# Who writes the low parts of the weight units during the two attentions

## The chip, the cores and the metric

One core of a Trainium2 chip runs the whole program. The time is device microseconds of one execution, from launch to end on that core.

## The reference

Two transformer blocks in a row, batch 1, 512 tokens, width 1024, all in float32. What matters here is the start of each block.

- Block 1: `h = rmsnorm(x)`, `proj = h @ w_in`. The first part of `proj` feeds a dilated window attention (12 heads in 3 groups), the second, after a shift by one token (`f + (f_prev - f) * mu`), an RWKV-7 scan, the third the gates. Then `merged @ w_out`, norm, and a feed-forward of 4096.
- Block 2: `proj = rms_norm(h) @ w_in`. It feeds a multiscale pooling, a banded attention with 8 query heads and a sink logit, and the gates. Then `merged @ w_out` and a gated feed-forward of 2816.

```python
logits = einsum(q, k) * scale + bias
p = exp(logits - lse); o = einsum(p, v)                    # block 1
p = exp(scores - m); denom = sum(p) + exp(sink - m)        # block 2
proj = h @ w_in                                            # both: float32 products
```

## The kernel before

**Weights.** All weights come as 126 units of 128 x 2048 float32 (1 MB), in a ring of three slots. A float32 product is made from three products of reduced precision: each unit is split into a high part and a low part, `w = hi + lo`, and so are the activations; line 524 multiplies high by high, 525 high by the activations' low part, 526 low by high. ScalarE writes the high part (`hi`, line 1092), GpSimd the low part, `raw - hi`, in place of the raw unit (line 515, all units in order but for ten). TensorE waits for it with `pe.wait_ge(*low_part(n))`. Ten units (20 to 29) in the RWKV stage have their low part from VectorE (`weights_low`, line 1738). Two semaphores count the low parts, `lo_ready` for GpSimd's and `lo_dve` for VectorE's.

**Order.** The order of each engine's work is written out by hand and each engine runs its own instructions strictly in that order; semaphores join them.

**The attentions.** Both run over items, one head and 128 queries each: 16 in the first attention (4 query tiles x 4 heads of the three groups, 384, 768, 1024, 1280 logits in turn), 32 in the second (256 or 384 logits). Per item:
- TensorE: the logits of item i+1, a fill of side work, *wait for the normalised logits of item i* (`prob_ready`), their transposes (line 601), a second fill, and the product with the values (line 609). The fills are pieces of weight products: 4 + 4 per item of the side columns (RWKV and gates) in the first attention, 2 + 2 per item of the gate columns in the second. A unit lasts two items in the first and four in the second.
- VectorE: scale and bias of the logits (1661, 1658), maximum (1665), for the second attention the sink (1667), the negated maximum (1668); then the hook `beside(i)`; then it waits for the exponential, adds the sink term (1672, second attention), takes the reciprocal (1673) and scales (1674), which releases the transposes. In the first attention the hook is `shift_item` (the token shift of a finished half, lines 1695 and 1696, at items 1 to 9 but for item 6); in the second it runs one step of the pooling.
- ScalarE: copies the transposes (1156), exponentials of item i+1 (1146, with a table load where the function before was another), a hook for the side work (1215, 1222, 1231 and 1528), the item's output (1162), and last the hook `after(i)`. In `after(i)` it writes the high part of a unit: at odd i of the first attention the unit `UNIT0["lora"] + i // 2 + 2` (so 11 after item 1, ..., 18 after item 15), at i = 3, 7, ..., 31 of the second the unit `UNIT0["gatep"] + i // 4 + 2` (78 after item 3, ..., 85 after item 31).

Of the kernel before, what the change touches and what calls it, by code (L numbers as in the profile page):

```python
# [12 lines left out]
ALU = mybir.AluOpType  # L13
# [30 lines left out]
RING = 3  # L44
# [12 lines left out]
UNIT0, USE0, UNITS, USES = {}, {}, {}, {}  # L57
# [108 lines left out]
def build(nc, x, wpack, lora_wa, lora_g, params, rel_bias, post_gains, sink, ctab, btab, icount, out):  # L166
# [7 lines left out]
    with ExitStack() as ctx:  # L174
        top = [nc.sbuf_base + (-nc.sbuf_base) % 64]

        def place(name, shape, dt=F32, at=None):
            size = 4 * int(np.prod(shape[1:]))
            if at is None:
                at = top[0]  # L180
                top[0] += size + (-size) % 64
            return nc.alloc_sbuf_tensor_at(name, shape, dt, offset=at), at + size + (-size) % 64

        def fixed(name, shape, dt=F32):
            return place(name, shape, dt)[0]
# [12 lines left out]
        def sem(name):  # L198
            return ctx.enter_context(nc.semaphore(name))
# [10 lines left out]
        raw = fixed("w_raw", [P, RING, UNIT])  # L210
        Wl = place("w_lo", [P, RING, UNIT], F32R, at=top[0] - 4 * RING * UNIT)[0]
        Wh = fixed("w_hi", [P, RING, UNIT], F32R)
# [106 lines left out]
        hi_ready, lo_ready, lo_dve = sem("hi_ready"), sem("lo_ready"), sem("lo_dve")  # L319
# [57 lines left out]
        source = packed_order()  # L377


        DVE_LO0, DVE_LO1 = UNIT0["rwkv"] + 2, UNIT0["rwkv"] + UNITS["rwkv"]  # L380

        def low_part(n):

            if n < DVE_LO0:
                return lo_ready, n + 1
            if n < DVE_LO1:
                return lo_dve, n - DVE_LO0 + 1
            return lo_ready, n + 1 - (DVE_LO1 - DVE_LO0)


        def half(pair, part):
# [30 lines left out]
        def f32(ap):  # L422
            return ap.bitcast(F32)

        def bank(b, n=512):
            return ps[:, b, 0:n]
# [27 lines left out]
        for h in range(Q_HEADS2):  # L454
            for qt in range(NT):
# [4 lines left out]
                n = (hi - lo) * P  # L460
# [7 lines left out]
        att = [dict(items=items1, LG=LG1, PT=PT1, first=0, banks=(7, 3), out_bank=2, outs=1),  # L468
               dict(items=items2, LG=LG2, PT=PT2, first=len(items1), banks=(6,), out_bank=7, outs=4)]
# [15 lines left out]
        @block.sync  # L485
        def _(sp):
            def load(n):
                if n >= RING:
                    sp.wait_ge(*freed[n - RING])
                sp.dma_start(raw[:, n % RING, :], wpack[source[n]]).then_inc(unit_in[n % RING], 16)  # L490

            xt = x.rearrange("(t p) d -> t p d", p=P)
            sp.dma_start(Xr[:, 0, :], xt[0]).then_inc(x_in[0], 16)
            sp.dma_start(C[:, 0:EARLY], ctab[:, 0:EARLY]).then_inc(ident_in, 16)
            for t in range(1, NT):
                sp.dma_start(Xr[:, t, :], xt[t]).then_inc(x_in[t], 16)
            sp.dma_start(PR[:], params).then_inc(params_in, 16)
            load(0)
            sp.dma_start(RB[0:N_BUCKETS, :], rel_bias).then_inc(rel_in, 16)
            sp.dma_start(BT[:], btab).then_inc(bucket_in, 16)  # L500
            load(1)
            sp.dma_start(C[:, EARLY:], ctab[:, EARLY:N_EARLY_CCOLS]).then_inc(consts_in, 16)
            for n in range(2, N_UNITS):
                load(n)

        @block.gpsimd
        def _(pool):


            for n in range(N_UNITS):  # L510
                if DVE_LO0 <= n < DVE_LO1:
                    continue
                slot = n % RING
                pool.wait_ge(hi_ready, n + 1)
                nc.gpsimd.tensor_tensor(Wl[:, slot, :], raw[:, slot, :], f32(Wh[:, slot, :]),  # L515
                                        ALU.subtract).then_inc(lo_ready, 1)
# [1066 lines left out]
        def _(dve):  # L1583
            order = Order(dve, dve_order)
            v = nc.vector
# [60 lines left out]
            def attention(a, beside):  # L1646

                items, first, LG = a["items"], a["first"], a["LG"]
                for i, it in enumerate(items):
                    st = 16 + 8 * (i % 2)  # L1650
                    mx, nmx, total, es, rec = (stat[:, st + c:st + c + 1] for c in range(5))
                    dve.wait_ge(lg_full, first + i + 1)
                    if i >= 2:
                        dve.wait_ge(pt_full, items[i - 2]["chunk1"])
                    for s in it["segs"]:
                        dst = LG[:, i % 2, s["off"]:s["off"] + s["n"]]
                        if "slope" in s:
                            ins = v.scalar_tensor_tensor(dst, s["bias"], s["slope"], bank(s["bank"], s["n"]),
                                                         ALU.mult, ALU.add)
                        else:  # L1660
                            ins = v.scalar_tensor_tensor(dst, bank(s["bank"], s["n"]), HD ** -0.5, s["bias"],
                                                         ALU.mult, ALU.add)
                    ins.then_inc(lg_read, 1)
                    dve.wait_ge(lg_read, first + i + 1)
                    order(v.reduce_max(mx, LG[:, i % 2, 0:it["n"]], AX.X))
                    if "sink" in it:
                        order(v.tensor_tensor(mx, mx, SNK[:, it["sink"]:it["sink"] + 1], ALU.max))
                    v.tensor_scalar(nmx, mx, -1.0, None, ALU.mult).then_inc(nmx_ready, 1)
                    beside(i)
                    dve.wait_ge(exp_ready, first + i + 1)  # L1670
                    if "sink" in it:
                        order(v.tensor_tensor(total, total, es, ALU.add))
                    order(v.reciprocal(rec, total))
                    v.tensor_scalar(LG[:, i % 2, 0:it["n"]], LG[:, i % 2, 0:it["n"]], rec, None,
                                    ALU.mult).then_inc(prob_ready, 1)
# [16 lines left out]
            def shift(n, dst, b, buf, mu):  # L1692

                dve.wait_ge(staged, n)
                v.scalar_tensor_tensor(dst[:, 1:T], ps[:, b, 1:T], OM[:, mu:mu + 1], buf[:, 0:T - 1], ALU.mult, ALU.add)
                v.tensor_scalar(dst[:, 0:1], ps[:, b, 0:1], OM[:, mu:mu + 1], None, ALU.mult).then_inc(shifted, 1)  # L1696
                dve.wait_ge(shifted, n)

            def shift_item(i):

                n = i - 1
                if n in (0, 1):
                    shift(n + 1, LTMP[:, n, :], n, G0[:, n, :], 24 + n)
                elif 2 <= n < GATE0 and n % 4 != 1:
                    pair, part = (n - 2) // 4, (n - 2) % 4
                    shift(2 + 3 * pair + part + 1, RKV[:, pair, part, :], n % 2, G0[:, n % 2, :], 8 * part + pair)
# [23 lines left out]

            def inc(ins, name):
                ins.then_inc(rs[name], 1)

            def weights_low(n):
                if DVE_LO0 <= n < DVE_LO1:
                    slot = n % RING
                    dve.wait_ge(hi_ready, n + 1)
                    v.tensor_tensor(Wl[:, slot, :], raw[:, slot, :], f32(Wh[:, slot, :]), ALU.subtract).then_inc(lo_dve, 1)

            def parts(c):  # L1740
                return (RKV[:, c % 2, j, :] for j in range(3))
# [300 lines left out]
            def pooling():  # L2042

                for g in range(4):
                    cur = Zp[:, g, :]
                    for lvl in range(g + 1):
                        left, right = (1, 0) if lvl == 0 else (2 ** (lvl - 1), 2 ** (lvl - 1))
                        dst = PW[:, lvl % 2, :]
                        order(v.tensor_tensor(dst[:, a0:b0], cur[:, a0 - left:b0 - left], cur[:, a0 + right:b0 + right],
                                              ALU.add))  # L2050
                        yield
                        cur = dst
                    mean = PW[:, (g + 1) % 2, 16:16 + T]
                    order(v.tensor_tensor(mean, cur[:, 16:16 + T], IC[:, g, :], ALU.mult))
                    yield
                    order(v.tensor_tensor(mean, mean, Zp[:, g, 16:16 + T], ALU.subtract))
                    yield
                    order(v.tensor_copy(PDh[:, g, :], mean))
                    yield
                    v.tensor_tensor(PDl[:, g, :], mean, f32(PDh[:, g, :]), ALU.subtract).then_inc(pd_ready, 1)  # L2060
                    dve.wait_ge(pd_ready, g + 1)
                    yield
# [1 line left out]
            dve.wait_ge(sink_in, 16)  # L2064
            dve.wait_ge(dist_in, 16)
            pool_work = pooling()
            attention(att[1], lambda i: next(pool_work, None))
            assert next(pool_work, None) is None
            for u in range(2):
                d = USE0["group"] + u  # L2070
# [106 lines left out]
```

## Time and profile before

| | us |
|---|---|
| median of three runs | 2262.39 (2260.95 to 2273.01) |
| profiled execution | 2259.61 |
| its span | 2257.8 |
| TensorE busy | 2058.6 (91%) |
| weight loads of TensorE busy | 1662.7 (74%) |
| VectorE busy | 856.9 (38%) |
| ScalarE busy | 791.4 (35%) |
| GpSimd busy | 533.4 (24%) |

PE is TensorE's matmuls, PEld its weight loads, DVE VectorE, ACT ScalarE, POOL GpSimd. A transpose is a matmul too, and the start of its weight load is when it could begin. The span is from the first to the last instruction; the execution's own time is 1.8 us longer. A row of a timeline gives the start and how long it took; what stands in brackets is the idle time before it and what ended it.

### The profile page before, as it was taken

How to read it: one execution, taken by the hardware profiler on the slowest of the kernel's cores; microseconds unless marked ns; L12 is line 12 of the kernel's file. 1: busy time of each engine (PE TensorE's matmuls, PEld its weight loads, DVE VectorE, ACT ScalarE, POOL GpSimd, SP SyncE). 2: the span in 40 equal slices, each digit the busy share in tenths (PEclk: the TensorE clock that was granted, in tenths of full speed). 3: DMA queues.
4: the chain of work that ended last, by engine and by line, in shares of the span. 5: the costliest groups of instructions: out<-in, count | busy, mean ns of one | idle time of the engine just before them, and what ended most of it. 6: DMA issues, size and time to landing. Idle time of an engine off the chain costs nothing.

```text
span 2257.8 us, 24099 instructions
## 1 busy us (share of the span) xinstructions
PE 2058.6 (91%) x10212; PEld 1662.7 (74%) x10212; DVE 856.9 (38%) x1437; ACT 791.4 (35%) x1140; POOL 533.4 (24%) x120
## 2 busy tenths in 40 slices
PE   6999969999999988998799989989988889999897
PEld 5877747778777877876688778767666677888786
DVE  2023335666666656522411144341553322111243
ACT  4235634435434423312422222242555223222222
POOL 2422210000000000013244434423122423444342
PEclk9999976989999886679799999989999998999999
DMA  4611210101001002013122222222111222322231
GB/s 150 221 56 61 80 63 1 45 21 43 27 22 45 24 20 98 1 47 112 65 93 94 98 89 94 94 79 80 40 55 59 91 69 74 108 95 93 75 97 71
DMA packets 31279, 160.77 MB, mean 71 GB/s; under 512 B 3103, under 2 KB 5535, under 8 KB 14916
## 3 DMA queue, kind: packets, MB, share of 16 engines
q1 hardware_dynamic: 19244, 135.40, 17.7%
q10 hardware_dynamic: 11928, 23.83, 3.1%
q8 instruction: 81, 1.33, 0.2%
q14 instruction: 26, 0.21, 0.0%
HBM read 152.63 MB, written 10.25 MB: 72 GB/s over the span
## 4 chain that ended last, share of the span: by engine, by line
PE 81%; DVE 9%; ACT 6%; issue 2%; POOL 1%; DMA 0%; POOLq 0%; ACTq 0%; DVEq 0%
PE ps L524 21%; PE ps L525 20%; PE ps L526 20%; PE ps L838 2%; PE ps L840 2%; PE ps L830 2%; PE ps L609 2%; PE ps L587 2%; ACT w_hi L1092 2%; POOL w_lo L515 1%; DVE level L1811 1%; PE ps L880 1%; PE ps L601 1%; DVE ht_lo L1602 1%; PE ps L870 1%
## 5 line engine op out<-in xcount | busy, mean ns | idle before, releaser
L515 POOL TENSOR_TENSOR w_lo<-w_raw,w_hi 128x2048 fp32r<-128x2048 f32 x116 | 533.2, 4597 | 1693.9 <-ACT w_hi L1092 1693.9
L524 PE MATMUL ps<-ht_hi,w_hi 128*128 128x512 f32 x1240 | 520.9, 420 | 36.7 <-DVE rkv L1696 22.3
L525 PE MATMUL ps<-ht_lo,w_hi 128*128 128x512 f32 x1240 | 496.9, 401 | 0.0
L526 PE MATMUL ps<-ht_hi,w_lo 128*128 128x512 f32 x1240 | 496.7, 401 | 0.0
L1092 ACT ACTIVATE w_hi<-w_raw 128x2048 fp32r<-128x2048 f32 x126 | 241.3, 1915 | 547.0 <-PE ps L526 532.3
L524 PEld LDWEIGHTS ps<-ht_hi,w_hi 128*128 128x128 f32 x1240 | 240.0, 194 | 119.3 <-issue 44.0
L526 PEld LDWEIGHTS ps<-ht_hi,w_lo 128*128 128x128 f32 x1240 | 240.5, 194 | 53.2
L525 PEld LDWEIGHTS ps<-ht_lo,w_hi 128*128 128x128 f32 x1240 | 241.2, 195 | 43.7 <-issue 1.4
L524 PE MATMUL ps<-w_hi,hid_hi 128*128 128x512 f32 x432 | 171.7, 397 | 24.2 <-DVE hid_lo L2026 16.4
L525 PE MATMUL ps<-w_lo,hid_hi 128*128 128x512 f32 x432 | 170.7, 395 | 0.0
L526 PE MATMUL ps<-w_hi,hid_lo 128*128 128x512 f32 x432 | 170.5, 395 | 0.0
L2026 DVE TENSOR_TENSOR hid_lo<-hidden,hid_hi 128x1024 fp32r<-128x1024 f32 x27 | 114.4, 4249 | 146.7 <-ACT hid_hi L1450 146.7
L524 PEld LDWEIGHTS ps<-w_hi,hid_hi 128*128 128x128 f32 x432 | 82.9, 192 | 43.3 <-issue 17.2
L524 PE MATMUL ps<-w_hi,ht_hi 128*128 128x512 f32 (+2 forms) x256 | 89.9, 351 | 25.4 <-DVE ht_lo L1991 17.6
L1314 ACT ACTIVATE tinv_t<-ps 128x512 fp32r<-128x512 f32 x96 | 57.7, 601 | 116.4 <-PE ps L840 116.4
L526 PEld LDWEIGHTS ps<-w_hi,hid_lo 128*128 128x128 f32 x432 | 82.7, 191 | 17.6
L525 PEld LDWEIGHTS ps<-w_lo,hid_hi 128*128 128x128 f32 x432 | 82.9, 192 | 17.2
L525 PE MATMUL ps<-w_lo,ht_hi 128*128 128x512 f32 (+2 forms) x256 | 89.3, 349 | 0.0
L526 PE MATMUL ps<-w_hi,ht_lo 128*128 128x512 f32 (+2 forms) x256 | 89.1, 348 | 0.0
L1811 DVE TENSOR_TENSOR level<-gram_inv,consts 128x512 fp32r<-128x512 f32 x112 | 80.4, 759 | 0.6
L2021 DVE TENSOR_TENSOR hidden<-ps,gate_act 128x1024 f32<-128x1024 f32 x16 | 19.6, 1224 | 159.9 <-ACT gate_act L1492 159.9
L1833 DVE TENSOR_TENSOR xinv<-ps,consts 128x512 fp32r<-128x512 f32 x96 | 62.4, 683 | 44.9 <-PE ps L830 44.4
(253 smaller groups left out, 2814.0 us busy)
## 6 DMA issues: line engine op xcount, KB each, us to landing
w_raw<-in_wpack SPq DMA_DIRECT2D x126, 1024.0 KB, 4.9
bias_skewed_dram<-bias_rows_dram ACTq DMA_DIRECT2D x1, 3840.0 KB, 22.9
toe<-bias_skewed_dram ACTq DMA_DIRECT2D x1, 3072.0 KB, 14.5
gate_dram<-gate_tile ACTq DMA_DIRECT2D x10, 256.0 KB, 4.8
x_res<-in_x SPq DMA_DIRECT2D x4, 512.0 KB, 6.7
merged<-gate_dram ACTq DMA_DIRECT2D x1, 2048.0 KB, 9.1
gate<-gate_dram ACTq DMA_DIRECT2D x1, 2048.0 KB, 14.1
x_res<-in_x ACTq DMA_DIRECT2D x1, 2048.0 KB, 9.9
```

The costliest lines, as they stand in the source:

```text
L515: nc.gpsimd.tensor_tensor(Wl[:, slot, :], raw[:, slot, :], f32(Wh[:, slot, :]), ALU.subtract).then_inc(lo_ready, 1)
L524: mm(dst, wh, ah, start=first, stop=False)
L525: mm(dst, wh, al, start=False, stop=False)
L526: return mm(dst, wl, ah, start=False, stop=last)
L587: last = mm(bank(s["bank"], s["n"]), s["q"], s["k"], start=True, stop=True)
L609: last = mm(out_slot(a, i), v, PT[:, j, :], start=j == 0, stop=j == len(it["vals"]) - 1)
L830: last = mm(ps[:, 4 + h, tok(t)], Mb[h][:, t, :], Tb[h][:, t, :] if lv else identR[:], start=True, stop=True)
L1092: actf(Wh[:, n % RING, :], raw[:, n % RING, :], ACT.Copy).then_inc(hi_ready, 1)
L1314: actf(TT[h][:].rearrange("p a b -> p (a b)"), bank(6 + h), ACT.Copy)
L1811: inc(v.tensor_tensor(Mb[h][:], GA[h][:], lmask(lv), ALU.mult), "m_ready")
L1833: inc(v.tensor_tensor(Xb[h][:], b3(4 + h), cast4(ident), ALU.add), "x1_ready")
L2026: v.tensor_tensor(HIl[:, 2 * g:2 * g + 2, :], HID[:, 2 * g:2 * g + 2, :], f32(HIh[:, g % RING, :, :]), ALU.subtract).then_inc(hid_lo, 1)
```

## The change

The units whose low part VectorE writes are now a list: units 11 to 17 in the first attention, 20 to 29 as before, 78 to 84 in the second. GpSimd skips them. In the first attention VectorE writes unit 9 + i/2 + 1 in the hook of item i = 2, 4, ..., 14, ahead of that item's shift; in the second unit 76 + i/4 + 1 in the hook of item i = 4, 8, ..., 28, behind that item's pooling step. `weights_low` waits for the unit's high part (`hi_ready`) and subtracts.

```diff
--- before.py
+++ after.py
@@ -377,15 +377,14 @@
         source = packed_order()
 
 
-        DVE_LO0, DVE_LO1 = UNIT0["rwkv"] + 2, UNIT0["rwkv"] + UNITS["rwkv"]
+        DVE_LOW = [*range(UNIT0["lora"] + 2, UNIT0["lora"] + 9),
+                   *range(UNIT0["rwkv"] + 2, UNIT0["rwkv"] + UNITS["rwkv"]),
+                   *range(UNIT0["gatep"] + 2, UNIT0["gatep"] + 9)]
 
         def low_part(n):
 
-            if n < DVE_LO0:
-                return lo_ready, n + 1
-            if n < DVE_LO1:
-                return lo_dve, n - DVE_LO0 + 1
-            return lo_ready, n + 1 - (DVE_LO1 - DVE_LO0)
+            by_dve = sum(u <= n for u in DVE_LOW)
+            return (lo_dve, by_dve) if n in DVE_LOW else (lo_ready, n + 1 - by_dve)
 
 
         def half(pair, part):
@@ -508,7 +507,7 @@
 
 
             for n in range(N_UNITS):
-                if DVE_LO0 <= n < DVE_LO1:
+                if n in DVE_LOW:
                     continue
                 slot = n % RING
                 pool.wait_ge(hi_ready, n + 1)
@@ -1696,8 +1695,16 @@
                 v.tensor_scalar(dst[:, 0:1], ps[:, b, 0:1], OM[:, mu:mu + 1], None, ALU.mult).then_inc(shifted, 1)
                 dve.wait_ge(shifted, n)
 
+            def weights_low(n):
+                if n in DVE_LOW:
+                    slot = n % RING
+                    dve.wait_ge(hi_ready, n + 1)
+                    v.tensor_tensor(Wl[:, slot, :], raw[:, slot, :], f32(Wh[:, slot, :]), ALU.subtract).then_inc(lo_dve, 1)
+
             def shift_item(i):
 
+                if i >= 2 and i % 2 == 0:
+                    weights_low(UNIT0["lora"] + i // 2 + 1)
                 n = i - 1
                 if n in (0, 1):
                     shift(n + 1, LTMP[:, n, :], n, G0[:, n, :], 24 + n)
@@ -1730,12 +1737,6 @@
 
             def inc(ins, name):
                 ins.then_inc(rs[name], 1)
-
-            def weights_low(n):
-                if DVE_LO0 <= n < DVE_LO1:
-                    slot = n % RING
-                    dve.wait_ge(hi_ready, n + 1)
-                    v.tensor_tensor(Wl[:, slot, :], raw[:, slot, :], f32(Wh[:, slot, :]), ALU.subtract).then_inc(lo_dve, 1)
 
             def parts(c):
                 return (RKV[:, c % 2, j, :] for j in range(3))
@@ -2064,7 +2065,13 @@
             dve.wait_ge(sink_in, 16)
             dve.wait_ge(dist_in, 16)
             pool_work = pooling()
-            attention(att[1], lambda i: next(pool_work, None))
+
+            def pool_item(i):
+                next(pool_work, None)
+                if i >= 4 and i % 4 == 0:
+                    weights_low(UNIT0["gatep"] + i // 4 + 1)
+
+            attention(att[1], pool_item)
             assert next(pool_work, None) is None
             for u in range(2):
                 d = USE0["group"] + u
```

## Rows read from the trace of the kernel before

**Rows 1.** The page, costliest groups: busy us, mean ns, idle before.
```profile
L515 POOL TENSOR_TENSOR w_lo<-w_raw,w_hi 128x2048 fp32r<-128x2048 f32 x116 | 533.2, 4597 | 1693.9 <-ACT w_hi L1092 1693.9
```

**Rows 2.** Lines view of VectorE, shapes apart: busy us, mean ns, idle before.
```profile
L1738 DVE TENSOR_TENSOR w_lo<-w_raw,w_hi 128x2048 fp32r<-128x2048 f32 x10 | 22.8, 2284 | 0.0
```

**Rows 3.** Stretch, length, busy us of PE, PEld, DVE, ACT, POOL; clock, DMA, GB/s.
```profile
134.00:297.00 163.00, 158.87 (x802) 121.95 (x800) 59.94 (x130) 84.12 (x123) 35.33 (x8) 0.98 0.19 65
1567.00:1747.00 180.00, 161.83 (x693) 108.60 (x694) 92.24 (x250) 93.59 (x193) 35.82 (x8) 0.94 0.14 49
```

**Rows 4.** Waits, 134 to 297 us: total us, times, longest.
```profile
PE ps L601 <- ACT probs_t L1156: 1.0, 4, 0.3
```

**Rows 5.** Waits, 1567 to 1750 us.
```profile
PE ps L601 <- DVE logits L1674: 15.2, 8, 2.4
```

**Rows 6.** Timeline of VectorE (start us, duration us), second attention, items 5, 6.
```profile
1598.76 1.92 DVE L1672 TENSOR_TENSOR stat<-stat 128x1 f32<-128x1 f32 x1 [3.28 <-ACT logits L1146]
...
1600.91 0.42 DVE L1674 TENSOR_SCALAR logits<-logits,stat 128x384 f32<-128x384 f32 x1
...
1602.61 0.15 DVE L1668 TENSOR_SCALAR stat<-stat 128x1 f32<-128x1 f32 x1
```

**Rows 7.** Timeline of GpSimd, second attention.
```profile
1596.12 4.54 POOL L515 TENSOR_TENSOR w_lo<-w_raw,w_hi 128x2048 fp32r<-128x2048 f32 x1 [25.09 <-ACT w_hi L1092]
```

**Rows 8.** Timeline of VectorE, first attention, items 4 and 6.
```profile
176.08 0.75 DVE L1695 SCALAR_TENSOR_TENSOR rkv<-ps,one_less_mu,side_tile 128x511 f32<-128x511 f32 x1 [6.54 <-ACT side_tile L1215]
...
177.00 0.16 DVE L1673 RECIPROCAL stat<-stat 128x1 f32<-128x1 f32 x1
177.19 0.42 DVE L1674 TENSOR_SCALAR logits<-logits,stat 128x384 f32<-128x384 f32 x1
...
193.55 0.75 DVE L1674 TENSOR_SCALAR logits<-logits,stat 128x1024 f32<-128x1024 f32 x1
```

**Rows 9.** Timeline of ScalarE, first attention.
```profile
156.60 1.90 ACT L1092 ACTIVATE w_hi<-w_raw 128x2048 fp32r<-128x2048 f32 x1
...
179.22 1.91 ACT L1092 ACTIVATE w_hi<-w_raw 128x2048 fp32r<-128x2048 f32 x1
...
196.04 1.91 ACT L1092 ACTIVATE w_hi<-w_raw 128x2048 fp32r<-128x2048 f32 x1
...
276.07 1.92 ACT L1092 ACTIVATE w_hi<-w_raw 128x2048 fp32r<-128x2048 f32 x1
```

**Rows 10.** Timeline of the weight loads, first attention: the transposes.
```profile
161.29 1.02 PEld L601 LDWEIGHTS ps<-consts,logits 128*128 128x128 f32 x8
...
181.70 0.48 PEld L601 LDWEIGHTS ps<-consts,logits 128*128 128x128 f32 x3
...
200.61 1.02 PEld L601 LDWEIGHTS ps<-consts,logits 128*128 128x128 f32 x8
...
279.24 1.02 PEld L601 LDWEIGHTS ps<-consts,logits 128*128 128x128 f32 x8
```

**Rows 11.** Timeline of ScalarE, second attention, items 3 and 4.
```profile
1594.13 1.91 ACT L1092 ACTIVATE w_hi<-w_raw 128x2048 fp32r<-128x2048 f32 x1
...
1596.32 1.28 ACT L1144 ACT_TABLE_LOAD   x1
...
1598.47 0.19 ACT L1146 ACTIVATION_READ_ACCUMULATOR logits<-logits,stat 128x1 f32 x1
```

**Rows 12.** Timeline of the weight loads, second attention: the transposes.
```profile
1594.50 0.37 PEld L601 LDWEIGHTS ps<-consts,logits 128*128 128x128 f32 x2
...
1601.38 0.31 PEld L601 LDWEIGHTS ps<-consts,logits 128*128 128x128 f32 x3 [2.31 <-DVE logits L1674]
```

**Rows 13.** Stretches after three of the waits; columns as rows 3.
```profile
1601.40:1607.50 6.10, 6.10 (x23) 4.14 (x23) 3.67 (x12) 1.77 (x5) 0.00 (x0) 0.72 0.01 3
1624.00:1628.50 4.50, 4.50 (x22) 3.29 (x23) 3.62 (x12) 1.76 (x5) 0.00 (x0) 1.00 0.00 0
1686.60:1693.80 7.20, 7.17 (x22) 4.90 (x23) 4.39 (x13) 1.76 (x5) 0.00 (x0) 0.60 0.01 2
```

## The prediction

> **What bounds the kernel now.** I read the page first: TensorE is busy for 91% of the span and holds 81% of the chain that ended last, so the rest of the machine matters only where it makes TensorE wait. The cost of the moved step comes next. GpSimd takes 4.60 us for one low part of a weight unit [rows 1]. VectorE already writes ten of them, in the scan stage, at 2.28 us each [rows 2]; GpSimd is idle there as it will be here, so I take that price. The change gives it 14 more: seven in the first attention (units 11 to 17) and seven in the second (78 to 84).
>
> Then I looked at the two stretches by themselves. From 134 to 297 us TensorE is busy for 158.9 of 163 us, from 1567 to 1747 us for 161.8 of 180; VectorE is busy for 59.9 and 92.2 us of them, GpSimd for 35 us in each [rows 3]. VectorE's low share looks like room for the new work. But a share does not say at which moment it is free, so the waits decide. In the first attention TensorE waits for nothing worth naming: the largest of its waits on the transposes is 1.0 us in all, for ScalarE's copies, and VectorE's normalised logits don't appear [rows 4]. In the second it waits for VectorE's normalised logits eight times, for 15.2 us [rows 5]. No wait of TensorE for GpSimd's low parts stands in either stretch: a unit is used two items (first attention) or four items (second) after it was split, so a faster low part is worth nothing by itself.
>
> **The change: what it removes.** 14 GpSimd instructions go. 14 x 4.60 = 64 us of GpSimd time is worth 0 on the path, since nobody waited for it. One side effect is worth something: in the second attention VectorE's one-column add of the sink term takes 1.92 us where it is blocked, from 1598.76 to 1600.68 [rows 6]. GpSimd's instruction began at 1596.12 and ran 4.54 us, to 1600.66 [rows 7]. The same add takes 0.16 us elsewhere. So 1.76 us are lost to the other engine each time, seven times, on the path (it stands between the exponential and the transposes for which TensorE waits). I take this out of the chain below.
>
> **What it adds: a wait in the middle of the softmax.** The new call stands in the hook that VectorE runs between the negated maximum and the wait for the exponential. Its first act is to wait for the high part of the unit from ScalarE. ScalarE writes that high part at the end of the *previous* item, after that item's output copy, and VectorE has no instruction that can pass it. Queued behind it are the shift (where the item has one), the reciprocal and the scale that releases the transposes on TensorE, and then the next item's logits. Idle VectorE time before the exponential is not what is filled; what counts is when the high part ends. In the first attention four of the seven items (2, 6, 10, 14) have 1,024 logits and three have 384.
>
> *First attention.* For item i the new start of the transposes is: end of the high part + 0.05 handover + 2.28 + 0.03 + shift (0.91 if there is one: 176.08 to 176.99) + reciprocal and scale (0.61 for 384 columns, 177.00 to 177.61; 0.95 for 1,024) + 0.06 [rows 2, 8]. Against the starts of now:
> - item 2: high part ends 156.60 + 1.90 = 158.50; new start 162.78, now 161.29: +1.49 [rows 9, 10].
> - item 4: 179.22 + 1.91 = 181.13; new 185.08, now 181.70: +3.38. This is the longest, as ScalarE does the LoRA activations before that high part.
> - item 6 (no shift): 197.95; new 201.32, now 200.61: +0.71.
> - item 14 (no shift): 277.99; new 281.36, now 279.24: +2.12.
> - items 8, 10 and 12 the same way from the same two views: +2.15, +0.60, +1.11.
>
> Sum 11.6 us. I followed the odd items too: there the exponential comes up to 3 us later than now, but VectorE is done before TensorE has finished its side pieces, so they neither add to it nor give anything back. TensorE has 2.5% of idle time in this stretch, so nothing absorbs a delay: its side pieces stand in a fixed order before the wait and cannot move behind it.
>
> *Second attention.* Take items 4 and 5. The high part ends 1594.13 + 1.91 = 1596.04 [rows 11]. Then 0.05 + 2.28 + 0.03, the add, the reciprocal and the scale (0.74 unblocked, 256 columns), and 0.05: transposes of item 4 at 1599.19, now 1594.50, so TensorE stands still for about 4.7 us where it did not before [rows 12]. Item 5 in turn: from the end of the scale to the negated maximum 1.43 (1601.33 to 1602.76 now) [rows 6]; table load and exponential 0.05 + 2.34 (1596.32 to 1598.66) [rows 11]; the three short operations 0.91 with the block taken out (1601.33 - 1598.66 - 1.76); 0.05 handover. Together 4.72 from transposes to transposes, so item 5 starts at 1603.91, now 1601.38: +2.53. That interval is about what TensorE needs by itself (4.5 [rows 13]), so the wait of now at item 5 is gone and item 4's is twice as long. In all seven repeats (the first is in the rows) the next item's transposes begin 5.33 to 5.35 us after the high part ends, so the term is the same: 7 x 2.53 = 17.7 us. The eighth wait of now, at the first item, stays.
>
> **TensorE's clock.** Now the granted clock is 1.00 after four of these seven waits of some 2.2 us, and below it after three: 0.72, 0.60 and again 0.72 of full speed, over 6.1, 7.2 and 6.1 us up to the next transposes, where an undisturbed interval is 4.5 us at 1.00 [rows 13]. These are stretches at the lower level (1.2 GHz in place of 2.4), and they cost 1.6, 2.7 and 1.6, together 5.8 us. The 4.7 us of idleness, twice as long, should bring such a stretch every time: 7 x 1.55 = 10.9, so 5.1 more, and a double one now and then; I take 5.7. In the first attention the mean is 0.98 [rows 3], with the loss at its very start. One stall of 3.4 us and two of 2.1 to 2.2 are new; counting the first as sure and the others at three in seven gives 1.9 x 1.55, some 2.7 us. Bounds for both: -2 (the clock falls as seldom as now, elsewhere it comes out better) and +19 (each of the seven costs 2.7 and four in the first attention 1.6: 18.9 + 6.2 - 5.8).
>
> **Sum.** 11.6 + 17.7 + 8.4 = 37.7 us on the profiled execution (2259.61 us, its span 2257.8 and 1.8 around it): 2297.3. The median of the runs shown is 2.8 higher, 2262.39, so the forecast is 2300.
>
> **Rivals.**
> - *The clock does not follow* (12%): only the order of waits counts, 29.3 us, 2292.
> - *The clock falls everywhere and twice* (13%): 29.3 + 19 = 48, 2311. For it: the 7.2 us interval. Against: it is one of three.
> - *Only the second attention pays* (6%): if TensorE's pieces in the first can run on while VectorE waits, 17.7 + 5.7 = 23, 2286. Against: they stand in front of the wait, and the starts follow them with no gap in front [rows 10].
> - *Faster: the port given back decides* (5%). All seven blocks go (7 x 1.76 = 12.3 us) and the new subtraction is hidden, with the 5.8 us of slow clock also back: 2262.4 - 18 = 2244. Its place is the add at items 5, 9, ... 29. It decides from the point where the high part is written at least 4.7 us earlier than now against the transposes (second attention) and 0.6 to 3.4 us (first). For it: the block is real. Against: ScalarE writes a high part only after the previous item's gate sigmoid and output copy, in program order.
>  The Trainium skill, "SBUF — State Buffer", section "SBUF: two separate sides", says an add of two SBUF inputs on VectorE and a GpSimd operation that reads SBUF lock each other out for a whole instruction; the trace agrees (1.92 us against 0.16). By that rule alone the change is a gain.
> - *No change* (4%): the delays are half of mine and the blocks give them back, 2262. It needs the exponentials to be late already at items 4, 8, ..., which the waits don't show.
>
> The forecast holds 60%. About 0.5% is what a measurement of this kernel tells from no change. Slower by more: 0.91, within: 0.04, faster: 0.05. The range: the 29 us of pure waits with some error gives 2286, the doubled clock 2313.
>
> **What would show it.** Right: GpSimd with 102 subtractions and VectorE with 24 at about 2.3 us; the add never above 0.2 us in the second attention; TensorE's wait for the normalised logits at items 2, 4, 6, ... of the first attention, the longest (3.4 us) at item 4; in the second some 4.7 us at items 4, 8, ..., 28 and next to none one item later; first stretch 11 to 16 us longer, second 18 to 30. Wrong: VectorE's subtraction beginning before the previous item's output copy, a wait that stays at items 5, 9, ..., or the granted clock at 1.00 behind the long waits.

## The result, and the profile after

The changed kernel takes 2304.1 us (median of four runs, 2301.12 to 2309.93), the kernel before 2267.7 in the same comparison (2260.95 to 2273.15). The ratio is 1.0165, with a 95% interval of 1.0124 to 1.0207: slower, by some 37 us. The forecast was 2300 us, 37.7 us more, in a range of 2286 to 2313. The profiled execution took 2303.82 us, with a span of 2302.0.

On the page the moved step looks harmless. GpSimd's group is down to 102 instructions, VectorE's is up to 24, at the same price as before [rows 1, 2]. The first lines are the page's busy times, the last two its costliest groups (busy us, mean ns, idle before).

```profile
PE 2077.2 (90%) x10212; PEld 1672.3 (73%) x10212; DVE 875.2 (38%) x1451; ACT 791.6 (34%) x1140; POOL 469.4 (20%) x106
...
L514 POOL TENSOR_TENSOR w_lo<-w_raw,w_hi 128x2048 fp32r<-128x2048 f32 x102 | 469.2, 4600 | 1802.1 <-ACT w_hi L1091 1802.1
...
L1702 DVE TENSOR_TENSOR w_lo<-w_raw,w_hi 128x2048 fp32r<-128x2048 f32 x24 | 54.9, 2288 | 102.0 <-ACT w_hi L1091 102.0
```

The new fact is in the last column: VectorE stands idle for 102 us in front of its subtractions, waiting for ScalarE's high part. Line 1738 had none of that [rows 2]. Most of this idleness costs nothing, as VectorE would have waited for the exponential anyway; what counts is what reaches TensorE. The two stretches, with the columns of [rows 3]; each is cut as there, at its new place:

```profile
134.00:308.00 174.00, 161.88 (x801) 122.50 (x799) 74.67 (x137) 84.19 (x123) 2.96 (x2) 0.97 0.18 61
1573.70:1790.10 216.40, 181.47 (x692) 121.14 (x693) 95.68 (x257) 93.53 (x193) 4.05 (x1) 0.83 0.12 41
```

The same matmuls take 11 us more in the first and 36 in the second. In the second the granted clock fell from 0.94 to 0.83. TensorE's waits for the normalised logits in the two stretches. The first had none; the second had 15.2 us [rows 4, 5], of which 2.4 us are the first item's, which the second line here leaves out (12.8 against 30.4 us):

```profile
PE ps L600 <- DVE logits L1673: 7.9, 6, 2.9
```

```profile
PE ps L600 <- DVE logits L1673: 30.4, 7, 4.5
```

One wait from close by, item 4 of the first attention: the high part (line 1091), the subtraction (1702), the scale (1673) and the transposes (600), from the timelines of ScalarE, VectorE and the weight loads. They answer to [rows 8 to 10].

```profile
180.33 1.90 ACT L1091 ACTIVATE w_hi<-w_raw 128x2048 fp32r<-128x2048 f32 x1
```

```profile
182.27 2.29 DVE L1702 TENSOR_TENSOR w_lo<-w_raw,w_hi 128x2048 fp32r<-128x2048 f32 x1 [11.07 <-ACT w_hi L1091]
...
185.58 0.42 DVE L1673 TENSOR_SCALAR logits<-logits,stat 128x384 f32<-128x384 f32 x1
```

```profile
162.55 0.86 PEld L600 LDWEIGHTS ps<-consts,logits 128*128 128x128 f32 x8 [1.39 <-DVE logits L1673]
...
186.05 0.50 PEld L600 LDWEIGHTS ps<-consts,logits 128*128 128x128 f32 x3 [3.28 <-DVE logits L1673]
...
206.90 0.85 PEld L600 LDWEIGHTS ps<-consts,logits 128*128 128x128 f32 x8 [0.62 <-DVE logits L1673]
...
290.33 0.86 PEld L600 LDWEIGHTS ps<-consts,logits 128*128 128x128 f32 x8 [2.04 <-DVE logits L1673]
```

VectorE was idle for 11.07 us, began 0.04 us after the high part ended (182.23), and TensorE stood for 3.28 us. The forecast for these four waits was 1.49, 3.38, 0.71 and 2.12.

In the second attention, item 8 and the two items behind it, from the timeline of the weight loads, and the stretches behind three of the seven waits (columns as [rows 3]; they answer to [rows 12, 13]):

```profile
1630.82 0.29 PEld L600 LDWEIGHTS ps<-consts,logits 128*128 128x128 f32 x2 [4.94 <-DVE logits L1673]
1638.92 0.22 PEld L600 LDWEIGHTS ps<-consts,logits 128*128 128x128 f32 x1
...
1644.18 0.48 PEld L600 LDWEIGHTS ps<-consts,logits 128*128 128x128 f32 x3
```

```profile
1605.80:1611.80 6.00, 5.96 (x19) 4.01 (x20) 3.77 (x10) 2.94 (x6) 0.00 (x0) 0.72 0.01 3
1630.80:1638.90 8.10, 8.08 (x19) 5.18 (x20) 4.39 (x13) 2.94 (x6) 0.00 (x0) 0.50 0.00 0
...
1767.50:1775.60 8.10, 8.07 (x19) 5.19 (x20) 3.46 (x11) 2.94 (x6) 0.00 (x0) 0.50 0.01 2
```

TensorE waits 4.94 us and then works all through the next 8.1 us, at the lower level (1.2 GHz). Item 5, 9, ... no longer waits, as forecast. But the interval behind a wait is 8.1 us in six cases of seven, where I had reckoned with the 4.7 us of a chain and one short slow piece of 1.55.

For all that follows I cut each profiled execution at the starts of the transposes: *first* is item 0 to item 15 of the first attention, *second* item 1 to item 31 of the second, *middle* what lies between the two. No edit touches the middle. The stretches come from one profiled execution each; the ratios come from 2 to 10 runs.

| kernel | first | middle | second | ratio to before (95%) |
|---|---|---|---|---|
| before | 145.3 | 1292.8 | 161.3 | 1 |
| changed | 156.3 | 1288.5 | 197.8 | 1.0165 (1.0124 to 1.0207) |
| first attention only | 156.3 | 1295.5 | 158.3 | 1.0035 (1.0009 to 1.0061) |
| second attention only | 145.3 | 1303.2 | 197.8 | 1.0173 (1.0137 to 1.0209) |
| one item later | 145.3 | 1292.6 | 142.8 | 0.9933 (0.9904 to 0.9962) |
| stall filled, 12 matmuls | 156.3 | 1298.6 | 171.8 | 1.0114 (1.0068 to 1.0160) |
| stall filled, 6 matmuls | 156.4 | 1295.7 | 187.3 | 1.0170 (1.0106 to 1.0234) |
| subtraction split | 156.3 | 1315.7 | 176.3 | 1.0180 (1.0108 to 1.0252) |
| wait only | 170.2 | 1292.7 | 200.0 | 1.0274 (1.0208 to 1.0340) |
| no low parts | 145.3 | 1303.0 | 143.2 | 0.9953 (0.9916 to 0.9990) |

The stretches say more than the ratios: over these ten profiles the middle, whose instructions are the same in all, runs from 1288.5 to 1315.7 us. That is TensorE's busy time at another granted clock, as the shortest and the longest show (changed kernel, then subtraction split; columns as [rows 3]):

```profile
298.60:1587.10 1288.50, 1170.59 (x6161) 958.45 (x6160) 573.38 (x927) 445.56 (x644) 230.30 (x50) 0.88 0.18 59
297.90:1613.60 1315.70, 1198.79 (x6161) 982.86 (x6160) 574.26 (x927) 446.10 (x644) 230.29 (x50) 0.86 0.17 58
```

The second stretch is not exact either: "before" and "first attention only" have the same instructions there and differ by 3.1 us (161.3 and 158.3), at a granted clock of 0.96 and 0.98. Costs and gains against "before" in that stretch are good to some 3 us.

### The profile page after: what moved, and what is told of

The parts are those of the page before. It is cut to its first block, busy times and chain, and to the rows that moved or that the text cites. A ratio compares the mean times of both kernels' runs of the same rounds, so it can differ in the third digit from the quotient of the medians.

```text
span 2302.0 us, 24099 instructions
## 1 busy us (share of the span) xinstructions
PE 2077.2 (90%) x10212; PEld 1672.3 (73%) x10212; DVE 875.2 (38%) x1451; ACT 791.6 (34%) x1140; POOL 469.4 (20%) x106
## 4 chain that ended last, share of the span: by engine, by line
PE 80%; DVE 10%; ACT 6%; issue 2%; POOL 1%; DMA 0%; POOLq 0%; ACTq 0%; DVEq 0%
PE ps L523 21%; PE ps L524 19%; PE ps L525 19%; PE ps L839 2%; PE ps L837 2%; ACT w_hi L1091 2%; PE ps L829 2%; PE ps L608 2%; PE ps L586 2%; PE ps L600 1%; DVE w_lo L1702 1%; DVE level L1812 1%; POOL w_lo L514 1%; PE ps L879 1%; DVE ht_lo L1601 1%
## 5 line engine op out<-in xcount | busy, mean ns | idle before, releaser
L514 POOL TENSOR_TENSOR w_lo<-w_raw,w_hi 128x2048 fp32r<-128x2048 f32 x102 | 469.2, 4600 | 1802.1 <-ACT w_hi L1091 1802.1
L523 PE MATMUL ps<-ht_hi,w_hi 128*128 128x512 f32 x1240 | 526.2, 424 | 36.2 <-DVE rkv L1695 21.7
L1702 DVE TENSOR_TENSOR w_lo<-w_raw,w_hi 128x2048 fp32r<-128x2048 f32 x24 | 54.9, 2288 | 102.0 <-ACT w_hi L1091 102.0
L1155 ACT ACTIVATE probs_t<-ps 128x384 f32<-128x384 f32 (+2 forms) x64 | 29.7, 483 | 163.3 <-PE ps L600 163.1
```

Source lines behind the costliest of these rows:

```text
L523: mm(dst, wh, ah, start=first, stop=False)
```

## The experiments

### The first attention alone

```diff
-                   *range(UNIT0["rwkv"] + 2, UNIT0["rwkv"] + UNITS["rwkv"]),
-                   *range(UNIT0["gatep"] + 2, UNIT0["gatep"] + 9)]
+                   *range(UNIT0["rwkv"] + 2, UNIT0["rwkv"] + UNITS["rwkv"])]
```

> Only the first attention's seven units go to VectorE; the second attention is as before. My theory (the wait for the high part holds up the softmax at items 2, 4, ..., 14): the first stretch is about 11 us longer than before, waits of 1.5, 3.4, 0.7, 2.1, 0.6, 1.1, 2.1 us, at most two slow-clock stretches, the second stretch as before (eight waits of about 2.2 us); ratio to before 1.004 to 1.007. Rival (the two attentions' costs hang together, or the cost is the clock of the whole kernel): more than 1.010 or within 0.2% of 1.

2270.18 us, median of ten, ratio 1.0035. Its first stretch is 156.3 us, as in the changed kernel; the second is 158.3, with the waits at items 5, 9, ... as before. My range for the ratio, 1.004 to 1.007, was a little high: 11.1 us are 1.0049, within the interval but above its middle. The rival that the two attentions' costs hang together falls.

### The second attention alone

```diff
-        DVE_LOW = [*range(UNIT0["lora"] + 2, UNIT0["lora"] + 9),
-                   *range(UNIT0["rwkv"] + 2, ...
+        DVE_LOW = [*range(UNIT0["rwkv"] + 2, ...
```

> Only the second attention's seven units go to VectorE. My theory: seven waits of 4.7 to 5.0 us, 17.7 us of pure waits more than before, and the rest of what the changed kernel's second stretch grew by (36 us) from the slow clock behind each; ratio to before 1.011 to 1.017. Rival (the clock in that stretch was slow by chance of phase after the first attention's shift): 1.008 to 1.010, with the granted clock near 1.00 after most waits.

Ratio 1.0173, just over the 1.017 that I had given as the upper end. The second stretch is 197.8 us, the changed kernel's to 0.02 us, with the granted clock at 0.83 again (columns as [rows 3]):

```profile
1579.00:1796.00 217.00, 181.87 (x694) 121.38 (x695) 95.75 (x257) 94.16 (x193) 4.25 (x1) 0.83 0.12 42
```

So the slow clock there doesn't come from a shift of phase by the first attention. The two costs add: 11.1 and 36.5 us in the kernels that have one of them, 11.1 and 36.4 in the changed kernel.

### The call one item later

```diff
-                if i >= 2 and i % 2 == 0:
+                if i >= 3 and i % 2 == 1:
                     weights_low(UNIT0["lora"] + i // 2 + 1)
...
-                if i >= 4 and i % 4 == 0:
+                if i >= 5 and i % 4 == 1:
                     weights_low(UNIT0["gatep"] + i // 4 + 1)
```

> All 14 units by VectorE, but the call stands in the hook of the item after (3, 5, ..., 15 and 5, 9, ..., 29), when ScalarE's high part has long been written or is just done. Same subtractions on the same engine, without the wait that holds the softmax up. My theory: no wait of TensorE for the normalised logits in the first attention; in the second the waits of about 2.2 us at items 5, 9, ... shrink to about 0.5 since GpSimd's block of 1.76 us is gone and the subtraction ends (1598.4 in the times of before) before the exponential (1598.7); ratio to before 0.991 to 0.996. Rival (the work itself on VectorE is what costs, 14 x 2.28 us): ratio 1.008 to 1.014.

2244.24 us, ratio 0.9933: this version beats both kernels. It writes the same 14 low parts on the same engine. VectorE's timeline at item 5 of the second attention:

```profile
1594.32 0.70 DVE L2050 TENSOR_TENSOR pool_tmp<-pool_z 128x528 f32<-128x528 f32 x1
1595.67 2.29 DVE L1702 TENSOR_TENSOR w_lo<-w_raw,w_hi 128x2048 fp32r<-128x2048 f32 x1 [0.65 <-ACT w_hi L1091]
1598.20 0.16 DVE L1671 TENSOR_TENSOR stat<-stat 128x1 f32<-128x1 f32 x1 [0.25 <-ACT logits L1145]
```

The subtraction waits 0.65 us for the high part and ends before the exponential. The add behind it takes 0.16 us, not 1.92 [rows 6]. TensorE's wait at item 5 is down to half a microsecond, and the stretch behind it is at full clock:

```profile
1599.07 0.31 PEld L600 LDWEIGHTS ps<-consts,logits 128*128 128x128 f32 x3 [0.46 <-DVE logits L1673]
```

```profile
1599.00:1603.60 4.60, 4.58 (x23) 3.30 (x23) 3.72 (x13) 1.76 (x5) 0.00 (x0) 1.00 0.02 4
```

The first stretch is 145.3 us, what it was before: there the move is worth nothing and costs nothing. All of the gain, 18.5 us, is in the second. "The work on VectorE is what costs" falls.

### The stall filled with matmuls

```diff
                     fill(2 * i)
+                    if first and i >= 4 and i % 4 == 0:
+                        for _ in range(WARM):                 # 12
+                            mm(bank(6), HTh[:, 0, 0:P], HTh[:, 0, :], start=True, stop=True)
                     pe.wait_ge(prob_ready, first + i + 1)
```

> The changed kernel, and at items 4, 8, ..., 28 of the second attention TensorE runs 12 extra matmuls of 128x512 into the bank of the transposes before it waits for the normalised logits; nothing reads them. They take 12 x 0.23 = 2.8 us of a wait of 4.7 to 5.0 us, so no wait gets longer. Theory that the idleness pulls the clock down: granted clock stays at 1.00 behind these waits, items 4 to 5 take 4.7 to 5.0 us in place of 8.1, the second stretch is 15 to 22 us shorter than in the changed kernel; ratio to before 1.007 to 1.010. Rival (the long intervals come from ScalarE's and VectorE's chain, the clock is a bystander): ratio as the changed kernel's, 1.015 to 1.018.

2285.37 us, ratio 1.0114, over my range of 1.007 to 1.010. The median is 19 us under the changed kernel's though TensorE does more; the intervals of the two ratios overlap, so I go by the stretch. The added matmuls of item 8 in TensorE's timeline, the wait that is left, and the stretches behind two waits:

```profile
1634.33 2.91 PE L597 MATMUL ps<-ht_hi 128*128 128x512 f32 x12
1639.01 0.44 PE L604 MATMUL ps<-consts,logits 128*128 128x128 f32 x2 [1.78 <-DVE logits L1677]
```

```profile
1615.50:1620.00 4.50, 4.44 (x19) 2.97 (x20) 3.01 (x10) 2.94 (x6) 0.00 (x0) 1.00 0.01 4
1639.00:1643.50 4.50, 4.49 (x20) 3.01 (x21) 2.73 (x9) 2.83 (x6) 0.00 (x0) 1.00 0.00 0
```

The transposes of items 4 and 8 stand where they did (9.25 and 9.53 us behind the item before, 9.24 and 9.52 in the changed kernel), but the next interval is 4.45 us in place of 5.99 and 8.11, at a granted clock of 1.00. The second stretch loses 26.0 us; I had said 15 to 22. The intervals behind the waits give 23.5 of them. The other 2.6 lie one interval later: in six of seven cases the changed kernel's clock was still low at its start, and it took 5.07 to 5.26 us in place of 4.74. Item 9's in the changed kernel:

```profile
1638.90:1644.20 5.30, 5.30 (x25) 3.81 (x24) 1.81 (x7) 1.65 (x5) 0.00 (x0) 0.89 0.00 0
```

The rival, that the long intervals are ScalarE's and VectorE's chain, falls: the chain fits into 4.45 us.

### Half of the filling

```diff
-WARM = 12
+WARM = 6
```

> The changed kernel with 6 extra matmuls (some 1.4 us) in each long stall of the second attention in place of 12; nothing reads them. About 3.3 us of idleness stay. Second stretch 197.8 us with none, 171.8 with twelve. If the clock's price follows the length of what is idle: 176 to 188 us, the granted clock low behind some of the seven. If any idleness over 2.5 us costs the whole price: 195 to 198. If activity anywhere in the wait is enough: 172.

The second stretch takes 187.3 us, inside the first range. The seven intervals behind the waits, which are 3.2 to 3.6 us now, are 5.98, 8.10, 4.45, 5.71, 4.45, 8.10 and 8.10 us. Two of them:

```profile
1638.70:1646.80 8.10, 8.09 (x19) 5.17 (x20) 4.38 (x13) 2.94 (x6) 0.00 (x0) 0.50 0.00 0
1666.00:1670.50 4.50, 4.45 (x19) 2.98 (x20) 3.01 (x9) 2.94 (x6) 0.00 (x0) 1.00 0.00 0
```

So none of the three answers holds for every wait: a wait of 3.30 us is followed by 4.45 us in two cases and by 5.98 in one, and one of 3.23 us by 8.11.

### The subtraction split

```diff
                 if i >= 4 and i % 4 == 0:
-                    weights_low(UNIT0["gatep"] + i // 4 + 1)
+                    n = UNIT0["gatep"] + i // 4 + 1
+                    if n in DVE_LOW:
+                        dve.wait_ge(hi_ready, n + 1)
+                        low_half(n, 0)                        # columns 0 to 1023
...                                                            # behind the scale of the same item:
+                    if first and i >= 4 and i % 4 == 0 and n in DVE_LOW:
+                        low_half(n, 1).then_inc(lo_dve, 1)    # the other 1024
```

> The changed kernel, but in the second attention VectorE writes only the first 1024 columns of a unit ahead of the exponential and the other 1024 behind the scale that releases the transposes. The wait at items 4, 8, ... falls from 4.7 to 3.5 us, and about 1.2 us of wait appears one item later, as the next item's logits come that much later: no gain in pure waits. So the second stretch (from the transposes of item 1 to those of item 31, 197.8 us in the changed kernel, 171.8 with the stall filled by matmuls) tells what the length of a stall does to the clock: if the price of the clock goes by the length of the single stall, 180 to 192 us; if any stall over 2.5 us costs the same, 196 to 200 us. Ratio to before 1.008 to 1.017.

The ratio, 1.0180, is over my range, and the second stretch, 176.3 us, is under both of the ranges that I had given (180 to 192 and 196 to 200), so neither answer about the clock holds. Its profiled execution has the longest middle of all (1315.7 us), which can hide the gain in a comparison of two runs; I go by the stretch. The waits are 3.5 to 3.9 us, 0.3 longer than with six matmuls, but six of the intervals behind them are 5.8 to 6.0 us and one 7.2:

```profile
1656.70:1662.50 5.80, 5.79 (x20) 3.90 (x21) 4.61 (x11) 2.94 (x6) 0.00 (x0) 0.75 0.00 0
```

The wait of 1.2 us that I expected one item later does not show. TensorE, slow for part of the interval, needs those 5.8 us by itself, and the later logits are hidden behind it.

### The wait alone, the subtraction on GpSimd

```diff
-        DVE_LOW = [*range(UNIT0["lora"] + 2, UNIT0["lora"] + 9),
-                   *range(UNIT0["rwkv"] + 2, UNIT0["rwkv"] + UNITS["rwkv"]),
-                   *range(UNIT0["gatep"] + 2, UNIT0["gatep"] + 9)]
+        DVE_LOW = [*range(UNIT0["rwkv"] + 2, UNIT0["rwkv"] + UNITS["rwkv"])]
...
-                    weights_low(UNIT0["lora"] + i // 2 + 1)
+                    dve.wait_ge(hi_ready, UNIT0["lora"] + i // 2 + 2)
...
-                    weights_low(UNIT0["gatep"] + i // 4 + 1)
+                    dve.wait_ge(hi_ready, UNIT0["gatep"] + i // 4 + 2)
```

> GpSimd subtracts all units of the two attentions again, as before; VectorE only waits for the high part at the same places as in the changed kernel. Theory A (the wait is all that hurts, and 2.28 us of subtraction are the rest of it): first stretch (transposes of item 0 to item 15, 145.3 us before) 1.1 us longer, second stretch with stalls of 2.4 us at items 4, 8, ... in place of those one item later; ratio 0.998 to 1.003. Theory B (a scale of two-port kind on VectorE is blocked by GpSimd's subtraction, which now starts at the same moment as VectorE wakes): the scale ends with GpSimd's instruction, first stretch 20 to 26 us longer than before, stalls of some 6.5 us in the second, which with the slow clock becomes 40 to 60 us longer than before; ratio 1.022 to 1.040.

2324.36 us, ratio 1.0274: theory B. GpSimd and VectorE are woken by the same high part. Item 4 of the first attention, GpSimd's timeline and VectorE's:

```profile
184.74 4.53 POOL L512 TENSOR_TENSOR w_lo<-w_raw,w_hi 128x2048 fp32r<-128x2048 f32 x1 [20.37 <-ACT w_hi L1089]
```

```profile
184.69 0.75 DVE L1692 SCALAR_TENSOR_TENSOR rkv<-ps,one_less_mu,side_tile 128x511 f32<-128x511 f32 x1 [11.08 <-ACT w_hi L1089]
185.36 0.21 DVE L1693 TENSOR_SCALAR rkv<-ps,one_less_mu 128x1 f32<-128x1 f32 x1
185.60 0.16 DVE L1670 RECIPROCAL stat<-stat 128x1 f32<-128x1 f32 x1
185.80 3.67 DVE L1671 TENSOR_SCALAR logits<-logits,stat 128x384 f32<-128x384 f32 x1
```

The scale of 384 columns, 0.42 us in [rows 8], takes 3.67 and ends 0.20 us after GpSimd's instruction (189.27). The shift, which reads PSUM and one SBUF tensor, and the reciprocal run freely. In the second attention it is the one-column add that is held, for 4.50 us at six of the seven items, up to the end of GpSimd's instruction (1622.09 + 4.50); at item 28 the add came first, in 0.16 us, and the scale was held:

```profile
1622.10 4.50 DVE L1669 TENSOR_TENSOR stat<-stat 128x1 f32<-128x1 f32 x1 [5.53 <-ACT w_hi L1089]
```

The first stretch grows by 24.9 us (20 to 26 expected), the second by 38.7, under the 40 to 60 that I expected. The slow clock cost less than I had allowed for. The waits are the longest of all, 6.3 to 7.1 us, and yet the interval behind them is 6.3 to 6.6 us in all seven cases, shorter than the 8.1 behind the changed kernel's 4.6 to 5.0. Behind item 8's wait of 7.07 us:

```profile
1654.90:1661.20 6.30, 6.30 (x19) 4.21 (x20) 3.40 (x10) 2.95 (x6) 0.00 (x0) 0.66 0.00 0
```

Given the wait at this place, it is better that VectorE subtracts, for 2.3 us, than that it meets GpSimd's 4.5.

### No low parts in the second attention

```diff
+        NO_LOW = range(UNIT0["gatep"] + 2, UNIT0["gatep"] + 9)
...
+            if n in NO_LOW:
+                return hi_ready, n + 1
...
-                wl = Wl[:, slot, :].rearrange("p (k c) -> p k c", k=kts)
+                wl = (Wh if n in NO_LOW else Wl)[:, slot, :].rearrange("p (k c) -> p k c", k=kts)
...
```

> The kernel before, with the low parts of units 78 to 84 left out: nobody subtracts, TensorE reads the high part in their place (as many matmuls; the gates and the pooling's projection are computed without the low part). This is what GpSimd's block costs, by itself. If the block of 1.76 us at items 5, 9, ..., 29 is what the version with the call one item later won: second stretch 139 to 144 us (142.8 there, 161.3 before), waits at items 5, 9, ... of about 0.5 us, granted clock 1.00; ratio to before 0.991 to 0.995. If that gain came from something else: above 155 us.

The second stretch is 143.2 us, with seven waits of 0.6 us at most; the kernel with the call one item later has 142.8. So that gain is the removal of GpSimd's block and of the slow clock behind the waits, and 2.3 us of subtraction in the right gap cost nothing. The ratio, 0.9953, is just above my range; the middle of its profile is 10 us longer than before's, which may be why.

## Why the prediction was right, and where it was off

**The price of the moved step.** Forecast 2.28 us, measured 2.288. That nobody waits for a low part earlier than before held.

**First attention, 11.6 us of waits.** The seven waits are 1.39, 3.28, 0.62, 2.06, 0.48, 1.01 and 2.04 us, together 10.9; forecast 1.49, 3.38, 0.71, 2.15, 0.60, 1.11 and 2.12. Each is about 0.1 us shorter than I reckoned. Of the clock I had put 2.7 us here (my 1.9 x 1.55 is 2.9, a slip); it fell once, behind item 4, where the interval to item 5 is 10.1 us and was 8.75: 1.4 us. Waits and clock make 12.3, yet the stretch grew by 11.1 (forecast 14.3 with the clock): the odd items, which I had at nothing, gave some back. The interval behind a wait is about 0.15 us shorter than before, 9.18 us behind item 2 for 9.33. The two waits of 2.1 us cost no clock.

**Second attention, 17.7 us of waits.** With the clock held at 1.00 by the filling, the stretch is 171.8 us. Before, with its own slow pieces taken out (6.12 - 4.57, 7.20 - 4.56, 5.19 - 4.74 and 6.10 - 4.56, together 6.2), it is 155.1. The waits are therefore 16.7 us. I was 1.0 over. The chain from the waiting item's transposes to the next is at most 4.45 us, not 4.72, which makes 1.9 less over the seven; 1.2 of it came back in the interval behind, which is 4.74 us and was 4.56.

**The clock, second attention: the term that was mis-sized.** I took 5.7 us more than before. Filling the stall takes 26.0 us away from the changed kernel's stretch, and before had 6.2, so it is 19.8 more. The second stretch grew by 36.4 us, outside the 18 to 30 that I had named as a sign of being right (the first by 11.1, inside its 11 to 16). What failed is the step from a wait's length to its price: I assumed one slow piece of 1.55 us for each wait, "a double one now and then", since the kernel before showed one double in three. Here six of seven intervals ran wholly at 0.50 of full speed, from 4.45 us to 8.10, and began the next one at it. The rival "falls everywhere and twice" had 2.7 us for each and was nearer for this stretch (18.9 - 5.8 = 13.1 more), still under it. Nor does the price grow with the wait: the waits of 6.3 to 7.1 us in "wait only" cost 1.9 to 2.1 us each in the next interval.

**Why the sum came out all the same.** By stretches the profiled pair differs by 11.1 + 36.4 = 47.5 us, less 4.2 in the middle and with 0.9 around them: 44.2. The comparison of all runs says 1.0165, some 37 us, and my 37.7 sits on that. The kernel before has scattered from 2249 to 2281 us over 13 runs of the last comparison; its profile, at 2259.61, is one of the faster ones. So the agreement within 4 us of the median is in part luck: in the stretches that the change touches, the sum was 10 us short (37.7 for 47.5). The mechanism is shown, the clock's size in the second attention was off by 14 us, and the interval of the ratio (28 to 47 us) holds 37.7 and 44.2 alike.

**The rivals.** "The clock does not follow" falls by the granted clock and by the filling. "Only the second attention pays" falls by the first attention alone. "The port given back decides" was wrong for this change, but its mechanism is real: the block is gone (VectorE's add is 0.16 us), and where the call doesn't hold up the softmax it is worth 18.5 us in the stretch, the 12.3 of seven blocks and 6.2 of slow clock. The Trainium skill ("SBUF — State Buffer", section "SBUF: two separate sides") says that a GpSimd operation that reads SBUF and began first shuts out a VectorE operation with two SBUF inputs, or one in a two-port mode, until it is done. The runs agree for the add of two SBUF inputs, by 1.92 and 4.50 against 0.16 us, and for a scale within SBUF, by 3.67 against 0.42; that the scale ran in such a mode no view says. For the clock it says, in "TensorE: Matmul & The Clock Gate", Part 1, that the clock is low after idleness until activity has been sustained; the traces agree, with 0.50 behind six idle waits of the changed kernel and 1.00 where they are filled. They do not let one read the price from the length of the wait.

**What stays open.** At which place a wait of 3.2 to 3.9 us must fall to cost 0, 1.5 or 3.65 us was not settled, nor why waits of 7 us cost less than waits of 4.8. In the changed kernel the waits from item 8 on, 27.1 to 27.6 us apart, all met the dear case.

## What to carry to other kernels

Work given to an idle engine costs what its *wait* costs, not its duration: find the moment at which its input is ready, and look at what is queued behind the call on that engine. Two places in one hook, one item apart, were 1.7% slower and 0.7% faster here, with the same instructions. Where a new wait leaves TensorE idle, give the slow clock behind it a range that reaches to the whole next interval at half speed and a little of the one behind (here 3.65 + 0.4 us behind a wait of 4.8), and not the mildest case that the old trace shows. Do not scale that price by the length of the wait: here the waits of some 7 us cost about 2 us each.

## What the runs showed of the hardware

- Added matmuls made a stretch faster: 84 of them, 2.9 us per wait, took 26.0 us off it; the granted clock stayed at 1.00.
- A one-column add on VectorE and a scale of 384 columns, both within SBUF, end with a GpSimd subtraction that runs beside them (1.92 or 4.50, and 3.67 us, in place of 0.16 and 0.42); an operation that reads PSUM and one SBUF tensor (0.75 us, as in [rows 8]) and a one-column reciprocal (0.16) are not held up.
- The price of a wait does not go by its length: behind waits of 3.2 to 3.6 us the next interval took 4.45 us twice and 8.10 us three times, behind waits of 6.3 to 7.1 us it took 6.3 to 6.6.
- A stretch of 1290 us whose instructions no edit touched differed by 27 us between profiled executions, with a granted clock of 0.88 in the shortest and 0.86 in the longest.
